# Two-block transformer stack on one core: TensorE multiplies a block of ones with itself inside eleven norms

## What is computed

```python
def rms_norm(x, g):                      # also _rmsnorm
    return x * rsqrt(mean(x * x, -1) + EPS) * g

# first block, layer l (x: 512 tokens; ctx: 256 tokens, feeds keys and values)
x = x + gt1 * merge_branches(z, y_conv, y_four, y_attn, ...)      # ... @ w_o
x = x + gt2 * (square(relu(modulate(x, g_norm2[l], sh2, sc2) @ w_ff1)) @ w_ff2)

# second block, layer l
h = _rmsnorm(x, pre_mix_g[l])
h = _ab_mixer(h, ...) if l % 2 == 0 else _mlstm_mixer(h, ...)
x = x + _rmsnorm(h, post_mix_g[l])
h = _swiglu(_rmsnorm(x, pre_ffn_g[l]), w_gate[l], w_up[l], w_down[l])
x = x + _rmsnorm(h, post_ffn_g[l])
```

## Time and profile before

| what | value |
|---|---|
| median of three runs | 3572.23 us (3572.21 to 3575.24) |
| the profiled execution | 3571.23 us, its span 3569.4 us |
| TensorE matmul busy | 3314.2 us, 93% |
| TensorE weight load busy | 2725.1 us, 76% |
| VectorE busy | 2112.5 us, 59% |
| ScalarE busy | 1261.0 us, 35% |
| mean granted TensorE clock | 0.951 |

### The profile page before, as it was taken

The page is one execution under the profiler, slowest core; times in us unless marked ns, Lnnn a source line. Parts: engine busy times, 40 slices in busy tenths (PEclk is TensorE's granted clock), DMA queues, the critical chain, the costliest instruction groups (busy, mean ns, idle before and its releaser), DMA issues.

```text
span 3569.4 us, 44839 instructions
## 1 busy us (share of the span) xinstructions
PE 3314.2 (93%) x16344; PEld 2725.1 (76%) x16344; DVE 2112.5 (59%) x2919; ACT 1261.0 (35%) x1808; POOL 0.2 (0%) x4
## 2 busy tenths in 40 slices
PE   6988999999999998999999999738999999989997
PEld 4878988777878887877778887517888777778886
DVE  7767885666565555665565555975333545653335
ACT  4554443554322223355322222233222245532221
POOL 0000000000000000000000000000000000000000
PEclk7999999999999998999999999858999989989998
DMA  6554542333222222222222322201222211113221
GB/s 218 188 185 152 182 160 96 112 113 107 91 80 99 96 95 93 84 82 83 89 83 94 99 95 82 71 7 64 101 94 95 94 65 48 48 59 100 94 99 66
DMA packets 99732, 353.67 MB, mean 99 GB/s; under 512 B 11792, under 2 KB 12944, under 8 KB 99600
## 3 DMA queue, kind: packets, MB, share of 16 engines
q1 hardware_dynamic: 99312, 350.82, 29.6%
q10 hardware_dynamic: 288, 1.05, 0.1%
HBM read 349.73 MB, written 2.10 MB: 99 GB/s over the span
## 4 chain that ended last, share of the span: by engine, by line
PE 84%; DVE 10%; ACT 3%; issue 2%; DMA 1%; SPq 0%; DVEq 0%; ACTq 0%
PE ring L1279 23%; PE ring L1281 23%; PE ring L1280 23%; PE ring L1531 2%; PE bank L1279 2%; PE bank L1320 2%; PE bank L1280 2%; PE bank L1281 2%; DVE w_lo L1967 1%; DVE z L2448 1%; DVE scr L2010 1%; DVE h_lo L2016 1%; ACT w_hi L698 1%; PE ring L1560 1%; PE ring L1561 1%
## 5 line engine op out<-in xcount | busy, mean ns | idle before, releaser
L1279 PE MATMUL ring<-h_hi,w_hi 128*128 128x512 f32 (+1 forms) x2896 | 1086.2, 375 | 42.0 <-DVE h_lo L2016 31.0
L1280 PE MATMUL ring<-h_lo,w_hi 128*128 128x512 f32 (+1 forms) x2896 | 1071.6, 370 | 0.0
L1281 PE MATMUL ring<-h_hi,w_lo 128*128 128x512 f32 (+1 forms) x2896 | 1070.5, 370 | 0.0
L1967 DVE TENSOR_TENSOR w_lo<-raw,w_hi 128x1024 fp32r<-128x1024 f32 x658 | 803.1, 1225 | 446.1 <-ACT w_hi L698 423.3
L698 ACT ACTIVATE w_hi<-raw 128x1024 fp32r<-128x1024 f32 x658 | 692.9, 1055 | 786.7 <-PE ring L1281 736.7
L1279 PEld LDWEIGHTS ring<-h_hi,w_hi 128*128 128x128 f32 x2896 | 552.2, 191 | 163.6 <-issue 40.6
L1281 PEld LDWEIGHTS ring<-h_hi,w_lo 128*128 128x128 f32 x2896 | 553.6, 191 | 91.8
L1280 PEld LDWEIGHTS ring<-h_lo,w_hi 128*128 128x128 f32 x2896 | 554.8, 192 | 84.0
L1279 PE MATMUL ring<-y_hi,w_hi 128*128 128x512 f32 (+1 forms) x1328 | 488.6, 368 | 39.4 <-DVE y_lo L1983 26.2
L1280 PE MATMUL ring<-y_lo,w_hi 128*128 128x512 f32 (+1 forms) x1328 | 486.1, 366 | 0.0
L1281 PE MATMUL ring<-y_hi,w_lo 128*128 128x512 f32 (+1 forms) x1328 | 485.9, 366 | 0.0
(11 more groups left out here) (301 smaller groups left out, 3144.9 us busy)
## 6 DMA issues: line engine op xcount, KB each, us to landing
raw<-ws SPq DMA_DIRECT2D x658, 512.0 KB, 3.3
x<-x_t SPq DMA_DIRECT2D x1, 2048.0 KB, 15.4
out_t<-x SPq DMA_DIRECT2D x1, 2048.0 KB, 7.3
xc<-ctx_t SPq DMA_DIRECT2D x1, 1024.0 KB, 10.3
z<-ropes ACTq DMA_DIRECT2D x2, 512.0 KB, 4.1
mat<-mats SPq DMA_DIRECT2D x1, 320.0 KB, 5.2
vec<-vecs SPq DMA_DIRECT2D x1, 216.5 KB, 2.6
v_bias<-bv SPq DMA_DIRECT2D x8, 0.5 KB, 7.4
```

What stands on the lines that cost most here:

```text
L1279: nc.tensor.matmul(o, a_hi, b_hi, start=start, stop=False)
L1280: nc.tensor.matmul(o, a_hi, b_lo, start=False, stop=False)
L1281: return nc.tensor.matmul(o, a_lo, b_hi, start=False, stop=stop)
L1967: nc.vector.tensor_tensor(w_lo[:, u, :], raw[:, u, :], f(w_hi[:, u, :]), ALU.subtract).then_inc(w_ready, 1)
```

## The change

A tuple `WARM = (22, 10, 18)` and a helper `keep_warm(first, n)` are added on TensorE. `keep_warm` issues n matmuls of the block of ones with itself, 128x128 by 128 columns, fp32r, into the first 128 columns of ring slot `(first + 1) % 4`, where `first` is the number of the next weight tile; nobody reads them. `column_norm` first waits until `post` has reached `first + 2`, that is until tile `first - 3`, the last user of that slot, has been read. Then it issues 22 such matmuls, then the sums, then 10, then it waits for the reciprocals and spreads as before, then 18. Nothing is removed, and no other engine's program changes.

```diff
+WARM = (22, 10, 18)
...
-            def column_norm(T, is_summed, spread):
-
+            def keep_warm(first, n):
+
+                for _ in range(n):
+                    nc.tensor.matmul(ring[:, (first + 1) % R, 0:P], ones_r[:, :], ones_r[:, :], start=True, stop=True)
+
+            def column_norm(first, T, is_summed, spread):
+
+                pe.wait_ge(post, first + 2)
+                keep_warm(first, WARM[0])
                 column_sums(T, is_summed, 2)
                 C.next(root_ready, T // P)
+                keep_warm(first, WARM[1])
                 spread_rstd(T, spread)
+                keep_warm(first, WARM[2])
...
-                    column_norm(length(stream), summed(kind, layer, stream),
+                    column_norm(first, length(stream), summed(kind, layer, stream),
```

## The result

| | before | changed |
|---|---|---|
| median, 8 runs each | 3573.42 us | 3584.48 us |
| lowest to highest | 3570.05 to 3575.24 | 3579.26 to 3586.76 |
| profiled execution, its span | 3571.23, 3569.4 us | 3583.08, 3580.8 us |

The ratio is 1.003 (95%: 1.0019 to 1.0041): the changed kernel is 0.3% slower, 11.1 us by the medians and 11.4 by the spans. The forecast was 3567 with a range up to 3580, so both the sign and the range missed.

What follows compares the result with a forecast made beforehand. TensorE, with 84% of the chain that ended last, was taken as the bound. Terms of +0.1, -0.8, -1.0, -0.5 and -2.7 us sum to -4.9: 3566.3 against the profile, 3567 against the median, range 3559 to 3580.

Steps and rivals of the forecast that it cites:

- near the edge in the joints with a table load ..., and good in the others: At all joints: fillers barely hold the full clock where 1.3 us stay idle over a table load, and hold it elsewhere.
- triples: Three places where a post norm is followed by a norm that sums again: -0.9 us each, -2.7 in all.
- the 40: In a triple, 18 fillers behind the first spread and 22 before the second sums, back to back: 4.5 us.
- rival (a) in part: Fillers fail to hold the clock in one triple or part of the joints: 3572 to 3582; chance 0.04 beyond the bound.
- (a) in full: Fillers do not hold the clock: about +7 us per triple, +4 at the other joints, 3597; chance 0.10.
- the 64: One-column matmuls of a triple's second sums: the clock falls inside them, 11.4 us for 13.8.
- pre_mix 0: Joint without a table load: spread gains 1.0 us; whether its sums run at half clock was left to the range.
- norm2 main: Two joints with a table load: spread gains 1.0 us if the clock holds, else 0; taken as -0.4 each.
- ctx joint: The norm2 with 256 columns: sums 0.5 us later, spread 1.22 to 0.6, 18 end 0.3 behind first block; +0.1.
- last post norm: Final joint: spread goes from 1.55 us, mostly at half clock, to 1.05; -0.5 us.
- (c): The clock never falls, not even in the 64: about -6.5 us per triple, -24 in all, 3548; chance 0.06.
- (b): Clock holds at every joint until some blocks into the 64, then comes back up: -10 us, 3562; chance 0.24.

Runs made afterwards that it cites:

- e_64: Changed kernel with each added matmul streaming 64 columns instead of 128, same counts; 3591.11 us, ratio 1.0049 to the kernel before.
- e_192: Changed kernel with each added matmul streaming 192 columns instead of 128, same counts; 3564.39 us, ratio 0.9972 to the kernel before.
- e_wait: Changed kernel with all three counts at zero, only the wait for post left; 3574.6 us, ratio 1.0002 to the kernel before.
- e_again3: Changed kernel unaltered, its fourth profile, one profiled run; 3564.89 us.
- e_dense: Changed kernel with 11, 5 and 9 added matmuls of 512 columns instead of 22, 10 and 18 of 128; 3560.27 us, ratio 0.9968 to before.
- e_first: Changed kernel with only 11 added matmuls of 512 columns ahead of the sums, other groups dropped; 3562.09 us, ratio 0.9968 to before.
- e_best: Changed kernel with 11, 4 and 9 added matmuls of 512 columns, none between a triple's second sums and spread; 3562.55 us, ratio 0.9969 to before.
- e_one22: Changed kernel without the 22 ahead of a triple's second sums; 3576.58 us, ratio 1.0004 to the kernel before.

## Why the prediction was wrong

**The step that failed** is "near the edge in the joints with a table load ..., and good in the others", under "Does the clock hold?". It gave the triples -0.9 us each. The triples' first parts, which have no table load, were as near the edge as the rest: in the changed kernel's profile the clock fell inside the first sums of triple 1 (at 2451.6), the 40 took 8.77 us where 4.5 were in the sum, and triples 1 and 2 cost +6.7 and +6.5. Three of the four profiles of this kernel have two such triples. The material for a better judgement was in the prediction: it said that a filler streams for about half of its 0.11 us, that L1880's matmuls stream twice as long (no row here measures that one), and that a stream of loads with one column holds nothing. It then took the earlier trace rows, L1880's run and a product paced by VectorE, as reason for "good". Neither row shows a continuous run of the thin kind. The right conclusion from rows was that nothing shown decides between the two, so that rival (a) in part deserved a large share. It got 0.04 beyond the bound and no chance of its own within it. In the profiles e_64 loses three triples, the change two, two, two or none, and e_192 none.

**The forecast asked for one behaviour at all three triples.** The runs show that one triple can be lost and the next not, and that the set changes between executions. With two lost of three the sum is: forecast -4.9, two triples at +6.6 rather than -0.9, which is +15.0, and 2.2 less gained at the other joints; together +12.3 of the 12.4. That case lay between rival (a) in part, which I ended at 3582, and (a) in full at 3597. The range's end at 3580 was set by that same 0.04.

**Rival (a)'s mechanism and prices were right in the triples.** From the start of the first spread to the first of the 64 there are 10.2 us (2454.52 to 2464.76), the "10 us behind the spread" that it named, against 4.9 before; that is +5.3 as it said. The second ten give +0.9 (from the first of the 64 to the second spread 15.8 us, before 14.9; forecast +1.0). Its first term, +1.1 for the ten, came out at +0.6 (last product to first spread 6.62 us, before 6.05), because the first sums took 1.41 us rather than the 1.87 of before; its words "first sums at full" misread that 1.87, which is mostly half clock. The sum it gave was +7; triples 1 and 2 have +6.7 and +6.5. Its +4 for the other joints came in no run: in e_64, where all three triples were lost, the other five add up to -0.7.

**What the forecast had right.** A filler costs 0.11 at the full clock (2.57 us for 22, 4.66 for 40) and 0.21 at half (8.77 for 40). The wait costs nothing (e_wait). Where the clock holds, the first of the 64 is 5.4 us behind the start of the spread (3170.42 to 3175.83), exactly the number given, the clock falls inside the 64, and they take 11.27, within the 11 to 12. That triple gained 1.1 where 0.9 was said, and the joints of e_again3, where none was lost, come out within 0.3 us of the whole sum. That agreement of the totals is partly luck: its triples gave -2.2, -1.2 and +0.4, and in the third the clock did fall ahead of the 40.

**The smaller joints.** pre_mix 0 gained 1.7 where 1.0 was said: its sums too were at the full clock (1.05 us), which had been left to the range. Its rows:

```profile
2198.95 1.05 PE L1332 MATMUL bank<-mat,scr 128*128 128x1 f32 x8
...
2201.08 1.16 PE L1339 MATMUL bank<-mat,small 128*128 128x128 f32 x8
```

norm2 main gained nothing where 0.4 each was a mean between two outcomes: the clock fell over the table load, 1.19 us of idle time stood ahead of the spread, and it ran at 1.2 GHz as before. In the ctx joint the same, and there it cost 1.5 rather than 0.1:

```profile
1002.00 2.08 PE L1339 MATMUL bank<-mat,small 128*128 128x128 f32 x8 [1.19 <-DVE small L2009]
...
328.79 1.22 PE L1339 MATMUL bank<-mat,small 128*128 128x128 f32 x4 [0.87 <-DVE small L2009]
329.67 4.08 PE L1312 MATMUL ring<-ones_r 128*128 128x128 f32 x18
```

The prediction had the ctx spread at 0.6 us and the 18 at 2.0; they took 1.22 and 4.08, and the first product waited for the 18. Its step 'the 18 end 0.3 behind the first block' took the full clock for granted where its own text called the joint near the edge. A dense stream gets these joints too: 0.9 us at each norm2 main in e_dense, 0.3 at ctx. At the last post norm the clock fell at the start of the spread, which took 1.95 us where 1.05 was forecast and 1.55 stood before; that joint cost 0.4 rather than gaining 0.5.

**The other rivals.** (c), that the clock never falls, came out nowhere: with the densest stream the 64 ran at half clock from 3.6 us on, so it isn't the fillers that could hold it there. The Trainium skill (TensorE: Matmul & The Clock Gate, Why this matters for your kernels) advises to keep TensorE busy, without idle gaps between bursts. The trace disagrees with the plain reading: 2.80 of 2.80 us busy at 0.50, while e_dense was busy for 4.50 of 4.50 us at 1.00. (b), 3562, is nearly what the dense versions give (3560 to 3564). Its clock that comes back behind the 64 is there in part: in e_dense's triples 1 and 2 it rose inside the second spread, which took 1.59 and 1.56 us rather than 2.08. That was not where the gain lay, as e_first, with a second spread of 2.07 us, has joints only 1.2 us longer; the first half was.

**What stays open.** Why one execution loses a triple and another doesn't was not settled. The instructions are the same and the fall comes at different places. The Trainium skill (same page, What's actually happening) says that the clock's monitor runs freely, so that the point of a transition depends on where the work falls in its period; that would fit, but no run here controls it. The traces narrow it down: counted from the start of the last product matmul, the clock fell after 3.6 to 3.7 us in the six lost triples, after 4.8 and 4.9 in the two in which it came back, and after 12.4 to 13.8, inside the 64, in the four that held. In e_64 it fell after 3.6 to 4.8 us and came back in none. The gain of pre_mix 0 in e_64 is open too. So is whether e_best is truly better than e_dense: 1.1 us of joints is less than the spread of the runs. And the stretches outside the joints differ by up to 6.3 us between the profiled executions (e_one22 against before), for a reason not looked into; there are half-clock spells there too, such as from 2929.2 to 2939.5 in before. The kernel before has 3567 to 3580 us over its runs, and I rest verdicts on joints and medians together.

## What to carry to other kernels

A filler meant to hold TensorE's clock did so here when it streamed for most of its time: 512 or 192 columns behind a 128-column load, or 128 behind a 32-column load, gained 0.3%, while 128 behind a 128-column load lost 0.1 to 0.3% at the same busy time. Put fillers only where an idle stretch takes them even at half clock; where two groups meet back to back in front of work that is waiting, they cost double when the clock is down. Where the clock comes out differently from place to place, take several profiles of the same kernel before believing any of them.

## What was unexpected on the chip

Under the change's stream the clock differed from execution to execution: the same groups ran at 1.00 or 0.50, triple by triple, and the device time of one unchanged program spread over 22 us (3565 to 3587, 19 runs), against 5.6 us for the dense one (6 runs). Also, 192 columns in place of 128 cost next to nothing in time while the clock is full (40 in 4.68 us against 4.66) and change the result from 0.1 to 0.3% slower to 0.28% faster; more columns behind the same load were free.
